# Two-layer hybrid decoder on one core: the router on the raw residual during the output projection, norm and splitting by 512 columns, a shorter routing chain, another assignment of weight rows

## The reference

```
mix = (heads' outputs) @ w_out                       # 2048 x 2048
h = layer_norm(ALPHA * h + mix, ln_mix_g, ln_mix_b)   # over the 2048 columns
ffn = moe_ffn(h, ...)
h = layer_norm(ALPHA * h + ffn, ln_ffn_g, ln_ffn_b)

def moe_ffn(x, router_w, router_bias, w_gate, w_up, w_down):
    aff = sigmoid(x @ router_w)                       # 16 experts
    sel = aff + router_bias
    # groups of 4 experts; the group with the best sum of its top two; in it the top two experts
    gate = aff[chosen] / sum(aff[chosen])
    h = silu(x @ w_gate[e]) * (x @ w_up[e]) * comb[e]  # every expert, 2048 -> 512
    return sum over e of h @ w_down[e]                 # 512 -> 2048
```

## Time and profile before

| | |
|---|---|
| runs, median (lowest to highest) | 1986.65 us (1986.45 to 1988.65) |
| the profiled execution, its own time | 1986.05 us |
| its span in the profile | 1983.7 us |
| mean granted clock of TensorE | 0.956 |
| busy: PE / PEld / DVE / ACT / POOL | 1749.8 / 884.8 / 506.8 / 285.0 / 17.7 us |
| read from HBM | 532.67 MB |
| mean of all transfers over the span | 270 GB/s |

### The profile page before, as it was taken

The page is one execution under the profiler, slowest core; times in us unless marked ns, Lnnn a source line. Parts: engine busy times, 40 slices in busy tenths (PEclk is TensorE's granted clock), DMA queues, the critical chain, the costliest instruction groups (busy, mean ns, idle before and its releaser), DMA issues.

```text
span 1983.7 us, 16590 instructions
## 1 busy us (share of the span) xinstructions
PE 1749.8 (88%) x6849; PEld 884.8 (45%) x6849; DVE 506.8 (26%) x955; ACT 285.0 (14%) x453; POOL 17.7 (1%) x36
## 2 busy tenths in 40 slices
PE   7999999999599888999869999979959998899884
PEld 5884444478343323333234454436834332343321
DVE  1201011445601111111160171324461111111115
ACT  1012011333310000000010001233331000000000
POOL 1000000000000000000000000000000000000000
PEclk9999999999699999999979999989979999999998
DMA  6343433282389999999972433327338999999995
GB/s 230 138 170 127 170 127 127 86 327 96 127 337 410 421 422 421 419 421 421 421 299 85 145 110 127 127 85 271 111 127 323 410 421 421 421 422 421 421 421 214
DMA packets 121327, 535.82 MB, mean 270 GB/s; under 512 B 12916, under 2 KB 12952, under 8 KB 70568
## 3 DMA queue, kind: packets, MB, share of 16 engines
q1 hardware_dynamic: 120680, 530.59, 67.5%
q0 software_dynamic: 576, 4.19, 0.5%
HBM read 532.67 MB, written 2.10 MB: 270 GB/s over the span
## 4 chain that ended last, share of the span: by engine, by line
PE 57%; issue 28%; DMA 8%; DVE 5%; ACT 2%; SPq 1%; POOL 0%; DVEq 0%; POOLq 0%
PE ps L662 22%; PE ps L861 8%; PE ps L644 6%; PE ps L915 4%; DMA ring<-in_moe_w_down 4%; PE ps L684 3%; PE ps L686 3%; PE ps L685 3%; DMA ring<-in_moe_w_up 2%; DMA arena<-in_moe_w_up 1%; PE ps L614 1%; PE ps L841 1%; PE ps L1009 1%; PE ps L842 1%; PE ps L850 1%
## 5 line engine op out<-in xcount | busy, mean ns | idle before, releaser
L662 PE MATMUL ps<-ring,hT 128*128 128x512 f32 x1024 | 441.7, 592 | 0.0
L662 PEld LDWEIGHTS ps<-ring,hT 128*128 128x128 f32 x1024 | 194.0, 190 | 239.9 <-issue 239.6
L1640 DVE TENSOR_TENSOR arena<-ps,arena 128x512 f32<-128x512 f32 x128 | 83.0, 685 | 412.9 <-PE ps L851 412.9
L861 PE MATMUL ps<-arena,hT 128*64 128x512 f32 x768 | 180.3, 625 | 8.3 <-issue 5.0
L915 PE MATMUL ps<-ring,arena 128*64 128x512 f32 x768 | 169.6, 594 | 9.2 <-DMA ring<-in_moe_w_down 9.2
L861 PE MATMUL ps<-arena 128*64 128x512 f32 x512 | 114.9, 596 | 21.5 <-DMA arena<-in_moe_w_up 10.7
L861 PE MATMUL ps<-ring,arena 128*64 128x512 f32 x512 | 114.5, 596 | 10.2 <-DMA ring<-in_moe_w_up 5.7
L861 PEld LDWEIGHTS ps<-arena,hT 128*64 128x64 f32 x768 | 57.3, 144 | 122.9 <-issue 120.2
L644 PE MATMUL ps<-hT,ring 128*128 128x256 f32 x512 | 110.8, 379 | 0.0
L1201 ACT ACTIVATE y_hi<-ps 128x512 fp32r<-128x512 f32 x64 | 36.5, 596 | 508.3 <-PE ps L851 266.6
L915 PEld LDWEIGHTS ps<-ring,arena 128*64 128x64 f32 x768 | 55.3, 137 | 120.7 <-issue 99.6
(11 more groups left out here) (278 smaller groups left out, 1420.8 us busy)
## 6 DMA issues: line engine op xcount, KB each, us to landing
arena<-in_moe_w_gate SPq DMA_DIRECT2D x48, 2048.0 KB, 18.3
ring<-in_moe_w_down SPq DMA_DIRECT2D x48, 2048.0 KB, 22.1
arena<-in_moe_w_up SPq DMA_DIRECT2D x32, 2048.0 KB, 20.5
ring<-in_moe_w_up SPq DMA_DIRECT2D x32, 2048.0 KB, 20.8
ring<-in_ab_w_in SPq DMA_DIRECT2D x24, 2048.0 KB, 7.9
ring<-in_moe_w_gate SPq DMA_DIRECT2D x16, 2048.0 KB, 20.7
arena<-in_moe_w_down SPq DMA_DIRECT2D x16, 2048.0 KB, 20.6
ring<-in_c_w_in SPq DMA_DIRECT2D x16, 2048.0 KB, 8.1
```

What stands on the lines that cost most here:

```text
L662: last = nc.tensor.matmul(tile(stage, i)[:, :], hT[:, 8 * u + k, tt * P:(tt + 1) * P], w[:, k, :], start=(u + k == 0), stop=(u == 1 and k ...
L861: last = nc.tensor.matmul(ps[bank][e * CAP:(e + 1) * CAP, :], xc(k)[:, at:at + CAP], w[:, e, kk, :], start=(k == 0), stop=(k == KT - 1), s ...
L1640: v.tensor_tensor(d, ps[6 + tt][:, :], d, ALU.add).then_inc(s["drained"][tt], 1)
```

## The change

Routing needs the layer norm of the residual, `(r - mean) * rstd * g + b`, times the router's weights W. After the change the kernel computes `r @ (g * W)` from the raw residual r, column chunk by column chunk, and corrects the 16 logits afterwards with `mean`, `rstd` and the column sums of `g * W` and `b * W`.

- **Start.** Two more DMAs bring gains and biases of the mixer's norms as 64 rows (L473), which PE transposes with the others; DVE makes `g * W`, `b * W` and their sums after the convolution, and PE adds these up over partitions with one product (`rsums`). Some constants are set first.
- **Output projection.** From the second chunk on, PE does eight transposes of the previous chunk's residual behind the first quarter, and four 32-row products with the router's weights behind the second. ACT copies one of the two raw tiles and DVE the other; DVE adds the partial logits up (`route_part`). The last chunk's part comes after the projection (`route`).
- **Norm and splitting** by 512 columns: columns 0 to 511 ahead of the routing chain or in it, 512 to 1023 behind it, and the other two after the first gathered tiles have been copied.
- **Routing chain.** The 32 transposes of the normed residual, its copies and the 16 router products are gone. Ranks come from all pairwise comparisons at once. The place's product (`pos`) is split into two tiles; the number of rounds is worked out after the first pair, and read by the engines after the first group. Sigmoid's and Silu's tables are asked for early. `acc` is scaled after the first pair.
- **Weight rows.** Gate and up rows are now taken as `512 * c + 4 * p + j`, so a step reads one block of 1 MB per expert without gaps, and a gathered tile takes every fourth of 512 columns of `h_hi` and `h_lo`.

The diff, cut:

```diff
-        gate_w = a["moe_w_gate"].rearrange("l e (p k) n -> l e p (k n)", k=KT)
+        gate_w = a["moe_w_gate"].rearrange("l e (c p j) n -> l e c p (j n)", c=4, j=4)
@@ SP
+            for n, w in enumerate((a["ln_mix_g"], a["ln_mix_b"])):
+                sp.dma_start(small_rows[at + 2 * KT * n:at + 2 * KT * (n + 1), :], w.rearrange("l (k p) -> (l k) p", p=P)).then_inc(small_loaded, 16)
@@ PE
+                    if c > 0 and part == 0:
+                        raw_transposes(lay, c - 1)
+                    if c > 0 and part == 1:
+                        route_part(lay, c - 1)
+            def raw_transposes(lay, c):
+                for tt in range(TT):
+                    t = first[f"out{lay}_{c}"] + tt
+                    pe.wait_ge(drained["D"], drained_by[:t + 1].count("D"))
+                    transposes(f"raw{lay}_{c}", tt, [h[:, tt, (4 * c + k) * P:(4 * c + k + 1) * P] for k in range(4)])
+            def route_part(lay, c):
...
+                for k in range(4):
+                    last = nc.tensor.matmul(tile(stage)[32 * k:32 * k + 32, 0:SEQ], scaled_w[:, 4 * c + k, :], rawT[:, k, :],
+                                            start=True, stop=True, skip_group_check=True)
...
-                pe.wait_ge(s["h_lo_ready"], TT)
                 group(0, True)
+                pe.wait_ge(routed, lay + 1)
@@ PE, gather_tile
+                    if first:
+                        pe.wait_ge(s["h_lo_ready"], TT * (k // 4 + 1))
+                    mine = slice(BANK * (k // 4) + k % 4, BANK * (k // 4 + 1), 4)
...
-                        nc.tensor.matmul(t, h_hi[:, tt, k * P:(k + 1) * P], pick8[:, tt, :], start=(tt == 0), stop=False)
+                        nc.tensor.matmul(t, h_hi[:, tt, mine], pick8[:, tt, :], start=(tt == 0), stop=False)
@@ ACT
+                for q in range(q0, 16):
+                    if q >= 6 and q % 4 == 2:
+                        raw_tile(lay, q // 4 - 1, 0)
+                    weight_hi(lay, q)
+                act.activation(rounds_f[:, 3:4], mhalf[:, 0:1], ACT.Sigmoid)
...
+                high(0, 0)
                 act.wait_ge(logits_ready, lay + 1)
+                act.activation(aff[:, :, :], logits[:, :, :], ACT.Sigmoid).then_inc(aff_ready, 1)
+                high(0, 1)
+                act.activation(rounds_f[:, 3:4], mhalf[:, 0:1], ACT.Silu)
+                for tt in range(TT):
+                    high(1, tt)
@@ DVE, residual
                 for c in range(4):
+                    if c > 0:
+                        raw_tile(c - 1)
+                    weight_lo(lay, 4 * c + 2)
+                    if c > 0:
+                        route_part(lay, c - 1)
+                    weight_lo(lay, 4 * c + 3)
+                    if c < 3:
+                        weight_lo(lay, 4 * c + 4)
+                        weight_lo(lay, 4 * c + 5)
@@ DVE, experts
+                centred(0, 0)
+                link(centred(0, 1))
+                route_part(lay, 3)
+                v.wait_ge(rstd_ready, 2 * lay + 1)
+                normed(0, 0)
...
+                v.tensor_copy(comb_g[:, :, :], comb_r[:, :, 0:GROUP])
+                low(0, 0)
+                v.wait_ge(psum_full, filled(f"pos{lay}", 0))
...
+                pick_half(0, 0)
+                v.wait_ge(psum_full, filled(f"pos{lay}", 1))
+                v.reduce_max(rounds_f[:, 0:1], tile(f"pos{lay}", 1)[:, 0:NE], AX.X).then_inc(drained["D"], 1)
+                pick_half(0, 1).then_inc(s["pick_ready"], 1)
+                low(0, 1)
+                norm(1)
+                for tt in range(TT):
+                    low(1, tt)
```

More of the change, by code:

```diff
@@ L1319, in _ @@
             attn_hi(3)
-            for q in range(1, 16):
-                weight_hi(1, q)
+            out_chunks(1, 1)
             experts(1)
```

370 lines of the change are left out of this document (232 added, 138 removed).

## The result

| | before | changed |
|---|---|---|
| median of the runs, us | 1987.65 (1986.45 to 1990.59, 4 runs) | 1945.6 (1941.08 to 1946.54, 4 runs) |
| profiled execution, span, us | 1983.7 | 1944.4 |
| out projection, layer 0 / 1, us | 89.8 / 91.4 | 95.7 / 97.3 |
| gap (residual's last piece to first expert product), us | 47.6 / 47.3 | 21.0 / 20.15 |

The ratio of the changed kernel's time to that of before is 0.9782, with a 95% interval of 0.9767 to 0.9797. The forecast was 1945. "Gap" means the same throughout: from the start of the residual's last piece on DVE to the start of the first expert product on PE.

What follows compares the result with a forecast made beforehand. The expert weight stream, held back once per layer by the gap, was taken to bound the kernel; start 0.9 + projections 12.0 - gaps 27.1 and 26.8 = -41.0, forecast 1945 us, own range 1938 to 1953, 8 in 10 1932 to 1961.

Steps and rivals of the forecast that it cites:

- What bounds the kernel: Expert weight stream sets the layer's end; bringing the first expert product forward starts the rest earlier by the same time.
- silent stretch: Window before the first expert product with DMAs idle because all six weight buffers are full: about 5 us instead of 35.
- The gap, 20.5: Residual's last piece to first expert product: 20.5 us, bounds 18 and 26, gaining 27.1 in layer 0, 26.8 in layer 1.
- The four tiles: First gathered product to first expert product: 6.3 us as before, plus 0.3 because DVE is late for the second tile.
- The projection, 6.0 a layer: Router work inside the output projection: transposes 1.4 and narrow products 0.6, so 2.0 us a chunk, 12.0 for both layers.
- The cover of 1.2 us: Output projection: DVE's split done about 5.8 us after the quarter's end, PE needing it at 7.0, leaving 1.2 us.
- The start, 0.9: Two added DMAs ahead of the last small transfer at the kernel's start cost 0.9 us, bounds 0 and 2.
- Stride and rows: Gather's strided weight load and the new weight-row pattern in the expert stream: both taken to cost zero.
- Late engines (1962): Rival: DVE and ACT late, gap 26 and PE stopping 1 us a chunk, 17 us lost; chance 0.13.
- faster or slower rows: Rivals: new row pattern speeds the expert stream to 428 GB/s (1935 us, chance 0.12) or slows it (2005, chance 0.04).
- the strided pace of 0.28 us: Rival: strided load spaces gathered products 0.28 us apart, 3.2 us a layer, 6.4 in all, time 1951; chance 0.12.
- the unreached stream: Rival: the six weight loads are not there when PE is, so the gain misses the stream, 1999 us; chance 0.01.

Runs made afterwards that it cites:

- e5: Changed kernel with the ranking of before (shifted comparisons, 35 small VectorE instructions) in place of the 17: 1950.3 us, ratio to before 0.9826.
- e7: Changed kernel with norm and splits of the second, third and fourth 512 columns all done ahead of the first copy of a gathered tile: 1967.7 us.
- e8: Changed kernel with 17 and 7 needless PE products around the counts, and norm and splits of the second 512 columns spread between gathered-tile copies: 1943.1 us.
- e3: Changed kernel with 12 needless PE products ahead of the wait for the mask and 6 behind the counts: 1944.8 us, ratio to before 0.9781.
- e10: Changed kernel with needless PE products, spread splits of the second 512 columns, and the router's work one quarter later in the projection: 1941.4 us.
- e9: Changed kernel with VectorE delayed by needless statistics instructions ahead of a split (layer 0) and the projection's router work done twice (layer 1): 1955.4 us.
- e1: Kernel before with only the new assignment of weight rows to partitions, splits packed so no strided load: 1985.3 us, ratio to before 0.9994.
- e2: Changed kernel with gathered blocks packed again, so ScalarE and VectorE read with the stride instead of PE: 1945.7 us, ratio to before 0.9790.
- e11: Changed kernel with needless PE products and all router transposes and narrow products behind the projection, with two buffers: 1941.0 us, ratio to before 0.9760.
- e12: As e11, with one VectorE centred piece moved from ahead of the last partial sum into the wait for the logit product: 1936.8 us.

## Why the prediction was right, by its own steps

- *What bounds the kernel.* Right. All of the gain is in the two gaps, the silent stretch shrank with them, and the stream kept its rate. A us in the chain to the first expert product is about a us at the end: gaps 2.9 us longer and the span 3.1 in e5, 18.9 and 21.0 in e7, 4.8 shorter and 4.1 in e8. The silent stretch was expected at about 5 us and is 8: the next transfer is issued 3.7 us behind the first expert product, after the change as before it, and 4 us from the end of the loads to that product (16.3 to 20.5) and 3.7 more make 8.
- *The gap, 20.5.* Measured 21.0 and 20.15. Each step up to the first gathered product came within 0.15 us. The four tiles were taken as 6.3 "as before", with 0.3 for VectorE. VectorE was in fact not late in layer 0, because PE gathered at half clock until 522 and took 7.5; in layer 1 it was late by the 0.3. The forecast's 6.3 held a clock that rose halfway, a fact of layer 0 in that execution and not of the work: layer 1 of the same trace had 7.4. That 20.5 lies between the two measured gaps is in part luck. e3 and e8 show the clock as the first limit and the copies as the second.
- *The projection, 6.0 a layer.* Measured 5.8 and 5.85: the sum is right and its parts are not. The eight transposes add 0.8 us and not 1.4 (in e10, where they don't wait, 1.03 from the product ahead to the product behind, of which 0.23 would pass anyway). They stand 0.11 apart; the forecast's 0.18 was read from a row of which the first us ran at half clock:

```profile
1342.00:1343.00 1.00, 1.00 (x6) 0.50 0.00 0
```

The narrow products add 0.66, near the forecast's 0.6, though the row it read for them is one of weight loads, 0.07 apart, and the eight instructions stand 0.055 apart. The rest, 0.4 to 0.45 a chunk, is the wait for the residual's second piece, which the forecast held to be covered by 0.1. Two errors of about half a us a chunk each cancelled, and that is luck.
- *The cover of 1.2 us.* Too small; like for like it is about 2.2, and VectorE can slip by 3.1 (e9). Its split was done 5.4 us after the quarter's end, not 5.8, and PE came 7.6 us after it, not 7.0.
- *The start, 0.9.* The first small-row transpose came at 20.59 in place of 19.86, and the projection 0.7 later.
- *Stride and rows.* Zero was right for the rows, which alone make 0.9994 (e1), and nearly right for the stride. The load did grow, to 0.309 us against the rival's assumed 0.28, but the spacing by 0.004 us and a group of four tiles by 0.3 (e2), about a third of the rival's price.
- *Left out.* About 1 us behind each gap. Most of layer 0's stands in layer 1's mixer, where no kernel of this study changes anything and which takes from 325.2 to 329.8 us, 327.8 before and 328.7 after; it goes with the mean granted clock, 0.95 in the shortest (e2) and 0.93 in the longest (e3). Behind layer 1's gap the strided load is a candidate: e2, which has it packed, took 494.8 us there and the changed kernel 496.6. These are single executions, and e9 and e10 have the strided load and took 495.3 and 495.65, so this is not shown.
- *The rivals.* Late engines (1962), faster or slower rows, the strided pace of 0.28 us and the unreached stream are each shown not to be what happened.

## What to carry to other kernels

A chain that holds back a DMA stream can be summed instruction by instruction from rows of similar shape, and each of its steps is worth its full length. But a stretch copied from the old trace carries that execution's clock with it: look at which level was granted before taking its length over. A row of transposes at half clock misled this forecast by half a us a chunk, and four gathered tiles at two clocks by 1.2 us in layer 0's gap. When work is moved out of a wait into a busy stage, price it in both places: here, by the marks of the traces, the router's work cost about the same inside the projection as behind it, and with a second buffer it was 1.7 us a layer cheaper behind (projection and gap of e11 against e8). Where a strided access can't be avoided, try it on the weight load, which has a product to hide behind.

## What was not expected of the hardware

- A strided weight load of 0.309 us beside products 0.235 us apart hardly slowed them (0.231 with a packed load of 0.188); what took longer were the first product after a wait, 0.46 against 0.34, and the third tile's first, 0.375 against 0.27.
- In the gap, with PE idle for a us here and a few us there, the granted clock fell to 0.50 and came back some us later, at other moments in the two layers of one trace. Twelve needless products were too few to hold it. Seventeen held it in both layers of e8 and e12 and in layer 0 of e10, but not in layer 1 of e10 nor in either layer of e11, where they ran into a dip, took 6.70 and 5.67 us in place of 4.04, and in e10 became the delay themselves.
- The same reads with a stride of 16 bytes cost ScalarE 1.14 us against 0.63 for 512 columns, and VectorE 1.09 against 0.69.
